# Four of eight gate pairs in the dense stage of a hybrid decoder layer, root, masks and tail reordered

## What is computed

```
h = RMSNorm(x);  proj = h @ w_in           # q|k|v, the RWKV columns, two gate inputs of 2048 columns
A = sliding-window attention (16 query heads, 4 key heads, window 128, ALiBi, sinks)
B = RWKV-7 time mixing (16 heads of 64, state S_t = S_{t-1}(diag(w) - kk^T (a kk)) + v^T k)
x += (sigmoid(gA) * (A @ w_branch_a) + sigmoid(gB) * (B @ w_branch_b)) @ w_out
x += MoE(RMSNorm(x))                       # 32 experts in 4 groups, top 1 group, top 2 experts, SwiGLU 512
out = RMSNorm(x)
```

## Time and profile before

| | us |
|---|---|
| median of 3 runs | 1751.11 (1749.46 to 1753.63) |
| the profiled execution | 1746.57 |
| its span, first to last instruction | 1744.8 |
| PE busy in it | 1502.7 (86%) |
| DVE busy | 702.1 (40%) |
| ACT busy | 395.3 (23%) |
| POOL busy | 38.1 (2%) |
| DMA | 529.28 MB, mean 303 GB/s |

### The profile page before, as it was taken

How to read it: one execution, slowest core, us unless ns; L and a number is a source line. 1 busy time by engine, 2 the same in 40 slices (tenths; PEclk the granted TensorE clock), 3 DMA queues, 4 the chain that set the end, 5 groups by cost and what they waited for, 6 DMA issues and landing times.

```text
span 1744.8 us, 26045 instructions
## 1 busy us (share of the span) xinstructions
PE 1502.7 (86%) x11408; PEld 900.3 (52%) x11408; DVE 702.1 (40%) x1052; ACT 395.3 (23%) x560; POOL 38.1 (2%) x34
## 2 busy tenths in 40 slices
PE   7999999999899899998977787787888876978775
PEld 6888988455646578885433242342333422423331
DVE  6666544547365566543323132222221312222223
ACT  5454444342142344443000000000000000000002
POOL 1000000001102010000000000000000000000000
PEclk9999999999999999998878788888888878878887
DMA  9655466331121384848999999999999999999994
GB/s 352 228 192 180 142 215 229 109 109 56 58 73 45 104 299 142 308 174 325 408 432 432 433 430 432 429 433 432 431 430 432 433 433 430 432 430 431 431 430 188
DMA packets 79832, 529.28 MB, mean 303 GB/s; under 512 B 7648, under 2 KB 9962, under 8 KB 65162
## 3 DMA queue, kind: packets, MB, share of 16 engines
q1 hardware_dynamic: 74912, 514.50, 72.3%
q0 software_dynamic: 2192, 9.35, 1.5%
q10 hardware_dynamic: 2650, 4.26, 0.6%
HBM read 521.80 MB, written 6.29 MB: 303 GB/s over the span
## 4 chain that ended last, share of the span: by engine, by line
PE 58%; DMA 29%; DVE 7%; ACT 4%; issue 2%; DVEq 0%; SPq 0%; ACTq 0%
DMA ring<-in_expert_w_up 16%; DMA ring<-in_expert_w_gate 11%; PE ps L908 10%; PE ps L1005 8%; PE ps L546 7%; PE ps L1085 6%; PE ps L1073 4%; PE ps L607 4%; PE ps L547 4%; PE ps L989 3%; PE ps L625 2%; DMA arena<-in_expert_w_up 2%; PE ps L997 1%; PE ps L509 1%; PE ps L815 1%
## 5 line engine op out<-in xcount | busy, mean ns | idle before, releaser
L1954 DVE TENSOR_TENSOR arena<-arena,ps 128x512 f32<-128x512 f32 x256 | 158.7, 681 | 318.6 <-PE ps L997 318.6
L1005 PE MATMUL ps<-arena 128*32 128x512 f32 x1024 | 149.0, 733 | 86.8 <-DMA arena<-in_expert_w_up 69.8
L546 PE MATMUL ps<-h_both,w_hi 128*128 128x512 f32 x544 | 190.3, 394 | 1.4 <-DVE w_lo L1559 1.4
L1005 PE MATMUL ps<-ring,arena 128*32 128x512 f32 x1024 | 133.9, 669 | 52.2 <-DMA ring<-in_expert_w_up 40.0
L547 PE MATMUL ps<-h_both,w_lo 128*128 128x256 f32 x544 | 152.9, 281 | 0.0
L625 PE MATMUL ps<-ring,arena 128*128 128x512 f32 x320 | 148.7, 606 | 0.0
L1073 PE MATMUL ps<-cst,arena 128*128 128x32 f32 x512 | 125.9, 403 | 15.2 <-ACT arena L1429 15.2
L1073 PEld LDWEIGHTS ps<-cst,arena 128*128 128x128 f32 x512 | 121.9, 328 | 22.8 <-ACT arena L1429 22.8
L1005 PEld LDWEIGHTS ps<-arena 128*32 128x32 f32 x1024 | 34.7, 130 | 190.3 <-issue 86.0
L546 PEld LDWEIGHTS ps<-h_both,w_hi 128*128 128x128 f32 x544 | 102.5, 188 | 24.2 <-DVE w_lo L1559 1.6
L1005 PEld LDWEIGHTS ps<-ring,arena 128*32 128x32 f32 x1024 | 33.0, 121 | 151.3 <-issue 77.4
(11 more groups left out here) (298 smaller groups left out, 1915.8 us busy)
## 6 DMA issues: line engine op xcount, KB each, us to landing
ring<-in_w_in SPq DMA_DIRECT2D x34, 2048.0 KB, 7.8
ring<-in_expert_w_down SPq DMA_DIRECT2D x16, 4096.0 KB, 33.4
ring<-in_expert_w_gate SPq DMA_DIRECT2D x16, 4096.0 KB, 30.0
arena<-in_expert_w_gate SPq DMA_DIRECT2D x15, 4096.0 KB, 30.0
arena<-in_expert_w_up SPq DMA_DIRECT2D x15, 4096.0 KB, 30.0
ring<-in_expert_w_up SPq DMA_DIRECT2D x15, 4096.0 KB, 35.1
arena<-in_expert_w_down SPq DMA_DIRECT2D x8, 4096.0 KB, 32.6
arena<-in_expert_w_down SPq DMA_DIRECT2D x16, 2048.0 KB, 30.3
```

Of the source, the lines that this page charges most:

```text
L546: mm(out, hi[:, 128 * n:128 * n + 128], both(k), start=start and n == 0, stop=False)
L1005: last = mm(ps[32 * c:32 * c + 32, bank, :], XS[:, k, 32 * j:32 * j + 32], w[:, HID * k:HID * k + HID], start=i == 0, stop=i == 3, tile_po ...
L1954: last = v.tensor_tensor(xs, xs, ps[:, banks[nb], :], ALU.add)
```

## The change

Block b = 3 of the gates joins the dense stage (GD = 4, banks 6 and 7). 128 filler steps remain: 56 in attention (11, 11, 17, 17 per unit), 36 in each half, none between the halves. In the halves four are moved or new: three of those ahead of line 735 now stand behind the transposes of v, and two single ones are put behind lines 842 and 847. Every filler tile now waits for the tile two before it to be taken. On ScalarE one gate_out leaves attention and each half's end, the second half's last one moves behind the first v_hi, and m_hi waits for the last gate step. The root moves ahead of the six exponentials. VectorE's masks of mt move ahead of the three writes of xt, and ScalarE's first level copy waits for xt. The chain of the picks' weights moves behind the first group's four scalings. In the last expert TensorE copies seven quarters of x into PSUM by products with the identity, an eighth ahead of the last scatter, and the scatters add to them; ScalarE squares and VectorE scales from PSUM. The last load is in three parts. The branch for over-full experts is adapted and left out here.

```diff
@@ -276,10 +276,10 @@
 UZ, UQ, UL, UM, UO = 48, 24, 6, 32, 32
-GD = 3
+GD = 4
...
 UX = UQ + UL + UG
-GD_BANK = (0, 2, 4)
+GD_BANK = (0, 2, 4, 6)
@@ -411,7 +411,8 @@
             sp.dma_start(place(i)[:, 0:SLOT], w[:, 0:SLOT]).then_inc(S("place3"), 16)
-            sp.dma_start(place(i)[:, SLOT:EW], w[:, SLOT:EW]).then_inc(S("last_half"), 16)
+            sp.dma_start(place(i)[:, SLOT:SLOT + 2048], w[:, SLOT:SLOT + 2048]).then_inc(S("last_half"), 16)
+            sp.dma_start(place(i)[:, SLOT + 2048:EW], w[:, SLOT + 2048:EW]).then_inc(S("last_quarter"), 16)
@@ -598,7 +599,7 @@
         if n == 0:
-            pe.wait_ge(*((S("qk_done"), 10), (S("va_done"), 2), (S("zs_done"), 5 + 24 + 3))[b])
+            pe.wait_ge(*((S("qk_done"), 10), (S("va_done"), 2), (S("zs_done"), 5 + 24 + 3), (S("zs_done"), 5 + 24 + 3))[b])
@@ -617,7 +618,7 @@
             n = NG + 2 * b + k // 8
-            if k == 0 and tile >= 2 * GD + 2:
+            if k == 0:
@@ -647,7 +648,7 @@
         last.then_inc(S("sc_ps"), 1)
-        gate_mm((10, 10, 17, 17)[u])
+        gate_mm((8, 8, 13, 13)[u])
@@ -722,19 +723,20 @@
         last.then_inc(S("half_ps"), 1)
-        gate_mm(4)
+        gate_mm(1)
...
         last.then_inc(S("half_ps"), 1)
+        gate_mm(3)
...
         last.then_inc(S("half_ps"), 1)
-        gate_mm(11)
+        gate_mm(9)
@@ -753,7 +755,7 @@
         last.then_inc(S("half_ps"), 1)
-        gate_mm(6)
+        gate_mm(3)
@@ -882,7 +886,7 @@
         last.then_inc(S("half_ps"), 1)
-        gate_mm(8)
+        gate_mm(4)
@@ -896,8 +900,6 @@
         last.then_inc(S("half_ps"), 1)
-        if hh == 0:
-            gate_mm(6)
@@ -991,12 +993,16 @@
-    def scatter(t, banks):
+    def scatter(t, banks, onto=False):
...
             last = mm(ps[:, banks[nb], :], CTB[32 * nb:32 * nb + 32, 128 * t:128 * t + 128], YS[32 * nb:32 * nb + 32, :],
-                      start=True, stop=True, tile_position=(32 * nb, 0))
+                      start=not onto, stop=True, tile_position=(32 * nb, 0))
         last.then_inc(S("scatter_ps"), 1)
...
+    def carried(t, nb, bank):
...
+        mm(ps[:, bank, :], C("ident"), x_sb[:, t, 512 * nb:512 * nb + 512], start=True, stop=False)
@@ -1077,10 +1083,18 @@
                 pe.wait_ge(S("ys_done"), g * 4 + j)
+            if last_group and j == GE - 1:
+                pe.wait_ge(S("adds_done"), 2 * NEXP - 2)
+                for nb in range(4):
+                    carried(0, nb, 4 + nb)
+                for nb in (0, 1, 3):
+                    carried(1, nb, nb)
...
                     pe.wait_ge(S("last_half"), g * 16 + 16)
+                if j == GE - 1 and k == 3:
+                    pe.wait_ge(S("last_quarter"), g * 16 + 16)
@@ -1092,13 +1106,13 @@
     pe.wait_ge(S("ys_done"), NEXP)
-    pe.wait_ge(S("adds_done"), 2 * NEXP - 2)
-    scatter(0, (4, 5, 6, 7))
-    scatter(1, (0, 1, 2, 3))
+    scatter(0, (4, 5, 6, 7), True)
+    carried(1, 2, 2)
+    scatter(1, (0, 1, 2, 3), True)
...
     with pe.If(over > 0):
-        pe.wait_ge(S("tail_add"), 8)
+        pe.wait_ge(S("tail_add"), 1)
@@ -1290,8 +1304,6 @@
         act.wait_ge(S("sm_done"), u + 1)
         f(probs[:, :, 0:w], probs[:, :, 0:w], ACT.Exp).then_inc(S("ex_done"), 1)
         f(aes[:, :], aes[:, :], ACT.Exp).then_inc(S("ex_done"), 1)
-        if u == 3:
-            gate_out()
@@ -1310,6 +1322,8 @@
         f(U(7), U(6), ACT.Square).then_inc(S("sq_done"), 1)
+        act.wait_ge(S("half_ps"), half_at("ks", hh))
+        f(U(11).rearrange("p (b n) -> p b n", b=2), ps[:, 2:4, :], ACT.Sqrt).then_inc(S("nrm_done"), 1)
@@ -1317,8 +1331,6 @@
         last.then_inc(S("P_done"), 1)
-        act.wait_ge(S("half_ps"), half_at("ks", hh))
-        f(U(11).rearrange("p (b n) -> p b n", b=2), ps[:, 2:4, :], ACT.Sqrt).then_inc(S("nrm_done"), 1)
@@ -1347,8 +1359,10 @@
                     act.wait_ge(S("wt_ps"), 10 * hh + 2 * (lv - 2) + hp + 1)
+                else:
+                    act.wait_ge(S("xt_done"), 12 * hh + 2)
                 f(U(14)[:, 512 * hp:512 * hp + 512], ps[:, hp, :], ACT.Copy).then_inc(S("v1_done"), 1)
-            if lv == 3 - hh:
+            if lv == 4 - hh:
@@ -1359,11 +1373,11 @@
         f(gn[:, 1, :], gn[:, 1, :], ACT.Sqrt).then_inc(S("gsd_done"), 1)
-        gate_out()
         if hh == 1:
...
+            act.wait_ge(S("chunk_used"), NG + 16)
...
             v_hi(0)
+            gate_out()
@@ -1431,7 +1445,7 @@
-                f(rstd[:, 0:2], rstd[:, 0:2], ACT.Sqrt).then_inc(S("sqrt_ready"), 1)
+                f(rstd[:, 0:2], rstd[:, 0:2], ACT.Sqrt)
@@ -1440,21 +1454,26 @@
-    def finish(turn):
+    for t in range(TT):
+        act.wait_ge(S("scatter_ps"), 2 * NEXP - 1 + t)
+        f(A(4096, 2048), ps[:, 4 - 4 * t:8 - 4 * t, :].rearrange("p b n -> p (b n)"), ACT.Square, accum_out=rstd[:, t:t + 1])\
+            .then_inc(S("top_sq"), 1)
+        act.wait_ge(S("ms_done"), 3 + t)
+        f(rstd[:, 2 + t:3 + t], rstd[:, 2 + t:3 + t], ACT.Sqrt).then_inc(S("rt_done"), 1)
...
+    def finish():
...
             t, nb = divmod(n, 4)
-            act.wait_ge(S("tail_add"), n + 1)
-            if n or turn:
-                act.wait_ge(S("tail_sq"), 8 * turn + n)
+            if n:
+                act.wait_ge(S("tail_sq"), n)
...
                 t = n // 7
-                act.wait_ge(S("ms_done"), 3 + TT * turn + t)
+                act.wait_ge(S("ms_done"), 3 + TT + t)
...
-    finish(0)
@@ -1722,6 +1741,10 @@
         step(v.tensor_tensor(g16(U(14)), g16(U(8)), tile16(C("lvlT", 64)), ALU.mult))
+        dve.wait_ge(S("half_ps"), half_at("mt", hh))
+        mt = ps[:, 0:4, :].rearrange("p b (g w x) -> p (b g) w x", g=4, w=2)
+        v.tensor_tensor(g16(U(10)), mt[:, :, 0, :], tile16(C("mU")), ALU.mult)
+        v.tensor_tensor(g16(U(11)), mt[:, :, 1, :], tile16(C("mUi")), ALU.mult).then_inc(S("mt_done"), 1)
@@ -1729,10 +1752,6 @@
         last.then_inc(S("xt_done"), 2)
-        dve.wait_ge(S("half_ps"), half_at("mt", hh))
-        mt = ps[:, 0:4, :].rearrange("p b (g w x) -> p (b g) w x", g=4, w=2)
-        v.tensor_tensor(g16(U(10)), mt[:, :, 0, :], tile16(C("mU")), ALU.mult)
-        v.tensor_tensor(g16(U(11)), mt[:, :, 1, :], tile16(C("mUi")), ALU.mult).then_inc(S("mt_done"), 1)
@@ -1947,34 +1966,34 @@
-    def added(t, banks, ev, quarters=range(4)):
...
-        for nb in quarters:
+    def added(t, banks, ev):
...
+        for nb in range(4):
...
             last = v.tensor_tensor(xs, xs, ps[:, banks[nb], :], ALU.add)
-            if ev == "tail_add":
-                last.then_inc(S(ev), 1)
-        if ev != "tail_add":
-            last.then_inc(S(ev), 1)
+        last.then_inc(S(ev), 1)
...
-    dve.wait_ge(S("rt_ex"), 2)
-    step(v.tensor_reduce(GS, GX, AX.X, ALU.add))
...
-    weighted(lambda at: slice(at, at + 1))
+    def picked_weights():
...
+        dve.wait_ge(S("rt_ex"), 2)
+        step(v.tensor_reduce(GS, GX, AX.X, ALU.add))
...
+        weighted(lambda at: slice(at, at + 1))
@@ -1983,6 +2002,8 @@
             gathered(q)
+        if first:
+            picked_weights()
@@ -2007,10 +2028,11 @@
-        dve.wait_ge(S("tail_sq"), 8 * turn + 4 * t + 4)
-        if t == 0:
-            dve.wait_ge(S("sqrt_ready"), 1)
-        step(v.tensor_reduce(rstd[:, t:t + 1], sspart[:, 4 * t:4 * t + 4], AX.X, ALU.add))
+        if turn:
+            dve.wait_ge(S("tail_sq"), 4 * t + 4)
+            step(v.tensor_reduce(rstd[:, t:t + 1], sspart[:, 4 * t:4 * t + 4], AX.X, ALU.add))
+        else:
+            dve.wait_ge(S("top_sq"), t + 1)
@@ -2018,31 +2040,31 @@
-    def last_scale(t, h):
+    def last_scale(turn, t, h):
...
         o = slice(1024 * h, 1024 * h + 1024)
-        v.scalar_tensor_tensor(out=fout[:, t, o], in0=x_sb[:, t, o], scalar=rstd[:, 4 + t:5 + t], in1=FW[:, o],
+        y = x_sb[:, t, o] if turn else ps[:, 4 - 4 * t + 2 * h:6 - 4 * t + 2 * h, :].rearrange("p b n -> p (b n)")
+        v.scalar_tensor_tensor(out=fout[:, t, o], in0=y, scalar=rstd[:, 4 + t:5 + t], in1=FW[:, o],
...
+        last_ms(turn, 0)
         last_rstd(turn, 0)
-        last_scale(0, 0)
+        last_scale(turn, 0, 0)
         last_ms(turn, 1)
-        last_scale(0, 1)
+        last_scale(turn, 0, 1)
         last_rstd(turn, 1)
-        last_scale(1, 0)
-        last_scale(1, 1)
+        last_scale(turn, 1, 0)
+        last_scale(turn, 1, 1)
...
     dve.wait_ge(S("fw_in"), 16)
-    dve.wait_ge(S("scatter_ps"), 2 * NEXP - 1)
-    added(0, (4, 5, 6, 7), "tail_add")
-    dve.wait_ge(S("scatter_ps"), 2 * NEXP)
-    added(1, (0, 1, 2, 3), "tail_add", (0, 1))
-    last_ms(0, 0)
-    added(1, (0, 1, 2, 3), "tail_add", (2, 3))
...
     with dve.If(over > 0):
+        for t in range(TT):
+            for nb in range(4):
+                last = v.tensor_copy(x_sb[:, t, 512 * nb:512 * nb + 512], ps[:, 4 - 4 * t + nb, :])
+        last.then_inc(S("tail_add"), 1)
```

More of the change, by code:

```diff
@@ L1466, in _ @@
                 act.wait_ge(S("fb_acc"), TT * NEXP + 1)
-                finish(1)
+                finish()
         @block.vector
@@ L1963, in _ @@
```

(14 more changed lines are left out.)

11 lines of the change are left out of this document (removed).

## The result

The changed kernel takes **1775.13 us** (median of 4 runs, 1770.58 to 1775.68) against 1750.28 (4 runs, 1747.64 to 1753.63) before: a ratio of 1.0135, 95% interval 1.0114 to 1.0156. It is slower by 24.9 us; 17.1 were forecast. The profiled execution took 1775.38 us (span 1773.6), 28.8 more than that of before. 3.6 of these arose ahead of the first dense product, in code that is the same: it starts at 239.86 here and at 236.28 before, and in ten more kernels that are alike up to there (those of the experiments) it started between 236.2 and 241.1.

The account below looks back on a forecast made before the run. It took TensorE's work ahead of the expert phase, which is bound by weight loads, to move the whole end. Its terms summed to +17.1 us on a 1751.1 median, giving 1768, range 1754 to 1780.

Parts of the forecast that it names:

- (a): Both halves' starts: the root ahead of the exponentials starts VectorE's chain 2.45 us sooner per half, -4.9 in all.
- (b): Both halves: masks of mt ahead of the xt writes and three fillers fewer bring 2.7 us per half, -5.4.
- (e): Chunk ends move: first half's levels lose an instruction wait and slow filler, -4.4; loads beside second half's states, +1.0.
- (c): First half's end: fillers there and behind it go, gaining 2.3 and 0.6 us, -2.8 rounded.
- (d): Second half's end: gate_out no longer stands ahead of m_hi, whose own 1.9 us are won, -1.9.
- tail: Last expert and output: identity products on the path net +6.2, shorter end with squares from PSUM -2.7, together +3.5.
- the clock term: Attention: longer TensorE idle times drop its clock; three waits cost 1.7 us each, +5.1, bounds 0 and 6.8.
- the bound of 4.4: Second half's states: upper bound of the +1.0 for a load adding one instruction wait like the 3.68 us one.
- rival 2: Attention: TensorE, not VectorE, sets the units' end, so removed fillers gain 10.4 us; whole -6.1, 1745; chance 0.07.
- rival 4: Attention: gate_out does not delay the Exp, only fewer fillers count; whole +9.4, 1760; chance 0.10.
- rival 1: No clock loss in attention, and the last expert's identity products cost nothing net; whole +5.8, 1757; chance 0.16.
- Rival 3: Second half's new loads hit instructions fully (+3.4), identity products stay at half clock (+6.0); whole +26, 1778; chance 0.12.

Follow-up runs that it names:

- the mended kernel: Changed kernel with gate behind the exponential, unused products in attention and between the halves, second half's load held, tail of before: 1746.83 us, ratio 0.9984.

## Why the prediction was right in the main, and 8 us too low

The steps in the order of time; "measured" is the difference of the two profiled executions over the stretch, in us (rounded, so the column adds up to 0.3 more than the whole):

| step | forecast | measured |
|---|---|---|
| fourth dense pair | +21.8 | +21.8 |
| Exp behind `gate_out`, units 1, 2, 3 | +1.7 +3.4 +2.6 | +1.7 +3.3 +2.5 |
| clock in attention | +5.1 | +6.2 |
| start of the first half (a) | -2.45 | -0.3 |
| masks of mt, first and second half (b) | -2.7 -2.7 | -3.1 -4.0 |
| first half's levels and states (e) | -4.4 | -4.4 |
| from the first half's end to the second (c) | -2.8 | -2.1 |
| **start of the second half (a)** | **-2.45** | **+3.3** |
| second half's levels | 0 | -1.7 |
| second half's states (e) | +1.0 | +3.7 |
| end of the second half (d) | -1.9 | -1.9 |
| merge and gather | 0 | +1.1 |
| picks | -2.6 | -3.4 |
| experts | 0 | -0.6 |
| tail | +3.5 | +3.4 |
| sum | +17.1 | +25.2 |

**The step that failed** is (c) with the clock term. It counted the fillers between the halves as a small gain ("2.3 and 0.6 us") and looked for the clock in attention alone. But those fillers filled a wait for VectorE, as attention's did: with them gone TensorE idles 1.14 and 4.51 us, and the granted clock is 0.50 for 20.5 us. That costs 5.8 us in the second half's start (17.74 against 11.92), which takes the root's 2.55 with it, and 0.7 between the halves (15.9 against 15.2 where the clock is whole there), which is what (c) lacks of its 2.8. The same rule that I applied in attention applied here, and I did not go through the timeline for every place at which fillers went. The kernel with products there shows it in part, and the mended kernel, whose clock is whole from 411 to 605 us, in full. What exactly lets the clock fall there stays open: in two kernels it fell while TensorE worked without a pause (below).

**The start of the first half** lost another 2.2 us to the lower clock at 424 to 431. This one comes and goes: two kernels that are the same up to there had full clock in it and a slower stretch earlier, of about the same cost; attention and this start together differ by 0.7 us. So the clock's cost is better summed over a stage than put to one place. With 6.2 + 2.2 + 5.8 the lower clock took 14.2 us in attention and the two starts, against 5.1 forecast. The merge's +1.1 may belong to it as well: its first products run at the lower clock, from 632.5 to 639.3, and before they did not.

**The load beside the states** came where it was expected and hit as hard as the bound of 4.4 nearly allowed (+3.7). I took +1.0, between nothing and the row's 4.4, as if it might not repeat. The experiment that held the load back shows that the load is what makes the wait; a load released into the states' 64x64 products should have been priced by that row nearly in full.

**Right**: the dense pair; that fillers in attention hide (rival 2 fell: attention with and without them is 79.2 and 78.6 us); that ScalarE's order would delay the Exp, to 0.1 us in each unit (rival 4 fell); that the waits of attention cost clock (rival 1 fell: clock loss in attention was 6.2, and filling the waits gave 6.3 back); the identity products on the path, net +5.7 against 6.2, with the shorter end at -3.6 against -2.7 and one more identity pair of 1.25 us between the scatters that I had put nowhere. Right too: the two new fillers in the states cost nothing net. Rival 3's first half came true, and the identity products did stay at half clock, but with 8.69 us they took no more than the 9.1 forecast. The second half's levels and masks came out 3.0 us better than forecast. In the levels 1.4 of the 1.7 us are waits without a cause in the profile, 0.19 us against 1.60. The other kernels of the changed order have 0.4 to 1.5 there, and take 31.5 to 33.1 us for these levels, where this one took 31.7 and before 33.4. So the gain repeats only in part. For the masks no run tells why.

**Luck.** The errors of the table are 13.5 us in the one direction (the clock in attention 1.1, the two starts 7.9, between the halves 0.7, the states 2.7, the merge 1.1) and 5.1 in the other (masks and levels 1.7 each, picks, experts and small ones). The sum is nearer than its terms.

The rule of the Trainium skill that I had set against the change, "TensorE: Matmul & The Clock Gate", part 1 (a throttled default that activity lifts), held here beyond what I gave it: by it work that computes nothing pays where TensorE would idle, and the trace agrees, with 6.3 us in attention. It does not agree everywhere: at 516 us of two kernels the clock fell while TensorE worked without a pause. Its section on oscillation names waits for a transfer; here the waits were for VectorE, with the DMA engines at 0 GB/s in two of the rows.

## What to carry to other kernels

Work that fills waits costs nothing where it stands; moved into the open it costs its whole time, and its old place may lose the clock as well. When fillers go, walk the timeline past every place where they stood and price each new wait by what TensorE does behind it. A change with many parts is worth taking apart: here root, order and picks, with one load held back, are worth 12.7 us on the kernel before, while the fourth dense pair alone costs 21.8 where it stands.

## What the runs showed of the hardware that was not expected

- A low clock can outlast a wait by far: the 20.5 us at 0.50 between and behind the halves hold the idle 4.51 us and then 14.4 us (525.98 to 540.4) in which TensorE worked without a pause, most of them products of 1 or 64 rows. In attention the stretches, begun inside waits of 4 to 7 us, were 6.8 us each.
- The clock can fall with no wait near it. In the kernel with five unused products it fell at 516.2, with no idle time over 0.19 us near it, in pairs of 256-column products of which every other one has 32 rows. In the kernel with the tail of before, which has no unused products, it fell in the same place:

```profile
512.00:516.10 4.10, 4.10 (x14) 1.87 (x14) 2.66 (x4) 2.74 (x4) 0.00 (x0) 1.00 0.72 276
516.10:520.30 4.20, 3.92 (x12) 2.18 (x11) 2.14 (x4) 1.09 (x1) 0.00 (x0) 0.50 0.01 3
```

What lets it fall there wasn't tried.
- Unchanged code ahead of the first dense product took 236.2 to 241.1 us in twelve executions, in steps that no part of a diff explains. Medians of few runs carry that too: the gate behind the exponential measured 13.7 us in the medians and 7.6 by the trace, which is that of its slowest execution (1767.88; the other three 1758.80 to 1762.92).
- A load moving 177 GB/s beside 64x64 products halted TensorE for 2.65 us with nothing to wait for. A load also ran beside the wait of 3.68 us in the first half of the kernel before, and in no half whose load was held back was there such a wait of over 1.5 us.
